# A two-layer decoder trunk: the router works on chunks of 128 neighbouring channels, its transposes stand between and behind the last output products, and its weights load from another queue

## What is computed

```
for l in range(DEPTH):                     # 2 layers
    h = rms_norm(x, norm_mix_g[l])
    x = x + token_mixers(h, ...)           # ends with merged @ w_out
    h = rms_norm(x, norm_ffn_g[l])
    glog = h @ rg_w + rg_b                 # 4 groups
    elog = h @ re_w + re_b                 # 32 experts, 8 in a group
    # best group, then the best two experts inside it; their weights from two softmaxes
    x = x + sum of w_e * (silu(h @ w_gate[e]) * (h @ w_up[e])) @ w_down[e] for the two experts
return rms_norm(x, norm_final_g)
```

## Time and profile before

| | us |
|---|---|
| median of 3 runs | 1450.69 (1449.82 to 1451.84) |
| the profiled execution, its own time | 1451.94 |
| its span, first to last instruction | 1450.2 |
| mixing half of layer 0, from the first `low` to the last add to x | 13.54 to 254.49 |
| router of layer 0, up to the gather of the first pair | 254.49 to 268.50 |
| experts of layer 0 | to about 720 |
| mixing half of layer 1, same marks | 729.76 to 970.99 |

### The profile page before, as it was taken

One profiled execution on the slowest core, in us unless ns is written; L12 is line 12 of the kernel. 1 busy time (PEld: TensorE's weight loads), 2 busy tenths in 40 slices (PEclk: granted clock), 3 DMA queues, 4 the chain that ended last, 5 costly groups with the idle time before them and its releaser, 6 DMA issues.

```text
span 1450.2 us, 17631 instructions
## 1 busy us (share of the span) xinstructions
PE 1391.4 (96%) x7295; PEld 837.9 (58%) x7295; DVE 559.5 (39%) x882; ACT 358.0 (25%) x532; POOL 6.3 (0%) x36
## 2 busy tenths in 40 slices
PE   6999999999999999999889999999999999999986
PEld 5899888644444444443378988885444444444432
DVE  6686645532222222221267757455222222222213
ACT  5554442311111111111155444431111111111101
POOL 0000000000000000000000000000000000000000
PEclk9999999999999999999989999999999999999998
DMA  7555757799999999999936457587999999999995
GB/s 273 191 193 177 256 204 279 285 422 421 421 421 422 420 421 422 420 421 421 404 133 218 157 192 269 195 335 286 421 421 421 421 421 421 421 421 420 421 421 212
DMA packets 101123, 490.18 MB, mean 338 GB/s; under 512 B 8716, under 2 KB 12084, under 8 KB 51892
## 3 DMA queue, kind: packets, MB, share of 16 engines
q1 hardware_dynamic: 99940, 488.72, 84.1%
q10 hardware_dynamic: 1104, 0.34, 0.1%
HBM read 487.98 MB, written 1.05 MB: 337 GB/s over the span
## 4 chain that ended last, share of the span: by engine, by line
PE 67%; SPq 18%; DVE 7%; DMA 4%; issue 2%; ACT 1%; DVEq 0%; ACTq 0%
PE psB L1619 20%; SPq L502 18%; PE psA L1367 13%; PE psB L1367 12%; PE psC L1630 10%; PE psA L1608 6%; DMA slot<-in_expert_w_down_dram 4%; DVE parts L926 2%; PE psA L1644 2%; PE psA L1645 1%; DVE score_work L1021 1%; DVE top L1020 1%; PE psD L1671 1%; ACT parts L731 1%; PE psC L1583 1%
## 5 line engine op out<-in xcount | busy, mean ns | idle before, releaser
L1619 PE MATMUL psB<-slot,uT 128*64 128x512 f32 x2048 | 460.0, 596 | 6.5 <-DMA slot<-in_expert_w_up_dram 6.5
L1619 PEld LDWEIGHTS psB<-slot,uT 128*64 128x64 f32 x2048 | 142.8, 137 | 275.1 <-issue 272.1
L1630 PE MATMUL psC<-slot,ybT_plain 128*64 128x512 f32 x1024 | 227.5, 596 | 3.9 <-ACT ybT_plain L839 2.7
L926 DVE TENSOR_TENSOR parts<-slot,parts 128x2048 fp32r<-128x2048 f32 (+1 forms) x80 | 177.4, 2249 | 70.2 <-ACT parts L731 69.9
L731 ACT ACTIVATE parts<-slot 128x2048 fp32r<-128x2048 f32 (+1 forms) x80 | 147.8, 1879 | 92.7 <-PE psA L1367 50.0
L1630 PEld LDWEIGHTS psC<-slot,ybT_plain 128*64 128x64 f32 x1024 | 71.1, 137 | 136.2 <-issue 129.3
L1242 DVE TENSOR_TENSOR x<-x,psA 128x1024 f32<-128x1024 f32 x62 | 75.7, 1221 | 190.2 <-PE psA L1645 190.2
L1367 PE MATMUL psB<-parts,hT_parts 128*128 128x512 f32 x448 | 138.9, 391 | 0.2
L1608 PEld LDWEIGHTS psA<-sel_mem,xn 128*128 128x128 f32 x1024 | 119.2, 192 | 27.0 <-issue 25.7
L1608 PE MATMUL psA<-sel_mem,xn 128*128 128x128 f32 x1024 | 127.4, 278 | 2.5 <-DVE sel_mem L1209 2.5
L1260 DVE TENSOR_TENSOR low_y_parts<-psC,low_y_parts 128x512 fp32r<-128x512 f32 x64 | 41.2, 686 | 223.7 <-ACT low_y_parts L842 223.7
(11 more groups left out here) (300 smaller groups left out, 1193.4 us busy)
## 6 DMA issues: line engine op xcount, KB each, us to landing
slot<-in_expert_w_gate_dram SPq DMA_DIRECT2D x128, 1024.0 KB, 23.1
slot<-in_expert_w_up_dram SPq DMA_DIRECT2D x128, 1024.0 KB, 22.4
slot<-in_expert_w_down_dram SPq DMA_DIRECT2D x128, 1024.0 KB, 24.3
slot<-in_w_in_dram SPq DMA_DIRECT2D x56, 1024.0 KB, 5.0
slot<-in_w_out_dram SPq DMA_DIRECT2D x8, 1024.0 KB, 4.9
slot<-in_w_proj_b_dram SPq DMA_DIRECT2D x4, 1024.0 KB, 5.0
slot<-in_w_proj_c_dram SPq DMA_DIRECT2D x4, 1024.0 KB, 5.0
slot<-in_w_proj_a_dram SPq DMA_DIRECT2D x4, 1024.0 KB, 4.9
```

The costliest lines, as they stand in the source:

```text
L926: v.tensor_tensor(low_part, mix_slot(i), high_part, ALU.subtract).then_inc(low_dve, 1)
L1619: ins = te.matmul(psB[j * BLK:(j + 1) * BLK, o, :], xT[:, 4 * half + c, j * BLK:(j + 1) * BLK], w[:, c, :], start=half == 0 and c == 0, st ...
L1630: ins = te.matmul(psC[j * BLK:(j + 1) * BLK, n, :], hidT[:, 2 * k + c, j * BLK:(j + 1) * BLK], w[:, c, n * 512:(n + 1) * 512], start=k == ...
```

## The change

It does four things.

1. **Chunks.** A chunk of the router is 128 neighbouring channels. The router's weights are loaded in that layout, `(c p) n` in place of `(p c) n`, which cuts each load into pieces of 4 or 32 numbers; before, a partition's piece was 8 times as long. The gain is multiplied into the router's weights `r_w` in `parameters()`, so that the copies out of PSUM are plain; for this the rows of `norm_ffn_g` come as a third small table.
2. **Loads.** `router_loads` is called by SP behind its sixth load of weights, and has seven DMAs; ACT issues none. The seven are waited for at the same place of `parameters()` as before.
3. **Sums.** x is added in four pieces, by half and token block, each as soon as its block of the output product is there.
4. **Transposes and products.** The 8 transposes of the first half of the channels stand between the token blocks of the last output product; 4 of t = 0 and 4 of t = 1 stand behind it, with the router's products in four groups among them. ACT makes four copies out of PSUM and DVE one. `spin` has 15 products in place of 14, and 4 more behind the ranking.

```diff
         for i in range(MIX_SLOTS):
             load_mix(i)
+            if l == 0 and i == RAWS - 1:
+                router_loads(sp)
...
-    def router_loads(act):
+    def router_loads(sp):
-            act.dma_start(g_ffn_all[:, :, :], norm_ffn_g.rearrange("l (p c) -> p l c", c=KC)).then_inc(router_landed, 16)
-            act.dma_start(rg_all..., router_group_w.rearrange("l (p c) n -> p l (c n)", c=KC)).then_inc(router_landed, 16)
-            act.dma_start(re_all..., router_expert_w.rearrange("l (p c) n -> p l (c n)", c=KC)).then_inc(router_landed, 16)
+            sp.dma_start(g_ffn_all[:, :, :], norm_ffn_g.rearrange("l (p c) -> p l c", c=KC)).then_inc(router_landed, 16)
+            for l in range(DEPTH):
+                sp.dma_start(rg_all[:, l], router_group_w.rearrange("l (c p) n -> l p c n", p=P)[l]).then_inc(router_landed, 16)
+                sp.dma_start(re_all[:, l], router_expert_w.rearrange("l (c p) n -> l p c n", p=P)[l]).then_inc(router_landed, 16)
...
 # DVE, parameters()
-        dve.wait_ge(router_landed, 16 * 5)
+        dve.wait_ge(router_landed, 16 * (3 + 2 * DEPTH))
-        v.tensor_copy(r_w[:, :, 0:NG], rg_all[:, bass.ds(l, 1), :, :].rearrange("p l c n -> p (l c) n"))
-        v.tensor_copy(r_w[:, :, NG:], re_all[:, bass.ds(l, 1), :, :].rearrange("p l c n -> p (l c) n"))
+        gain = cols[:, FFN_COLS + l * KC:FFN_COLS + (l + 1) * KC].unsqueeze(2)
+        v.tensor_tensor(r_w[:, :, 0:NG], rg_all[:, l], gain.to_broadcast([P, KC, NG]), ALU.mult)
+        v.tensor_tensor(r_w[:, :, NG:], re_all[:, l], gain.to_broadcast([P, KC, NE]), ALU.mult)
...
 # ACT, router_norm()
-        act.wait_ge(dve_out, (l + 1) * len(on_dve))
+        for t in range(NT):
+            act.wait_ge(routeT_ps, l * 5 + t + 1)
+            turned(psC[:, t, :], 0, 4, t)
+        act.wait_ge(x_mixed, l * 2 + 2)
         sc.activation(xn[:, 0:D], x[:, 0, :], ACT.Square, accum_out=ss[:, 0:1]).then_inc(ss_act, 1)
-        even_bank(psA, 0, hT, g_ffn)
+        turned(psD[:, 0, :], 4, 4, 0)
+        turned(psD[:, 1, :], 4, 2, 1)
         root_of(2)
-        even_bank(psB, 2, hT, g_ffn)
...
 # DVE, router_norm() and the adds
-        for b, ps in ((1, psA), (3, psB)):
-            v.tensor_tensor(hT[:, 2 * b:2 * b + 2, :], ps[:, 1, :]..., g_ffn[...]..., ALU.mult).then_inc(hT_dve, 1)
+        dve.wait_ge(routeT_ps, l * 5 + 5)
+        v.tensor_copy(hT[:, 6:8, P:S], psC[:, 0, 0:2 * P].rearrange("p (c s) -> p c s", c=2)).then_inc(routeT_dve, 1)
...
-            v.tensor_tensor(dst, dst, result(n)[:, :, :], ALU.add).then_inc(dve_out, 1)
+            dve.wait_ge(out_ps, l * 2 + half + 1)
+            v.tensor_tensor(dst[:, 0, :], dst[:, 0, :], (psA, psB)[n % 2][:, 0, :], ALU.add).then_inc(x_mixed, 1)
+            v.tensor_tensor(dst[:, 1, :], dst[:, 1, :], result(n)[:, 1, :], ALU.add).then_inc(dve_out, 1)
...
 # PE, inside the last output product, and behind it
+                if part == 1 and t == 0:
+                    ins.then_inc(out_ps, 1)
+                    if half == 1:
+                        pe.wait_ge(dve_out, ...)
+                        for u in range(NT):
+                            route_transposes(psC[:, u, :], range(4), u)
...
+        pe.wait_ge(x_mixed, l * 2 + 2)
+        route_transposes(psD[:, 0, :], range(4, 8), 0)
+        for t in range(NT):
+            pe.wait_ge(routeT_act, l * 4 + t + 1)
+            route(0, t)
+        pe.wait_ge(dve_out, (l + 1) * len(on_dve))
+        route_transposes(psD[:, 1, :], (4, 5), 1)
+        route_transposes(psC[:, 0, :], (6, 7), 1)
+        pe.wait_ge(routeT_act, l * 4 + 3)
+        route(1, 0).then_inc(route_ps, 1)
+        pe.wait_ge(routeT_act, l * 4 + 4)
+        pe.wait_ge(routeT_dve, l + 1)
+        route(1, 1).then_inc(route_ps, 1)
+        spin(15)
```

More of the change, by code:

```diff
@@ L275, in build_trunk @@
         thresholds = sb("thresholds", [P, S // BLK - 1])
-        rows = sb("rows", [DEPTH * (KC + CONV * 4), P])
-        cols = sb("cols", [P, DEPTH * (KC + CONV * 4)])
+        FFN_COLS = DEPTH * (KC + CONV * 4)
+        rows = sb("rows", [FFN_COLS + DEPTH * KC, P])
+        cols = sb("cols", [P, FFN_COLS + DEPTH * KC])
         g_mix = sb("g_mix", [P, KC])
@@ L383, in build_trunk @@
         vm_ps = sem("vm_ps")
+        out_ps = sem("out_ps")
+        routeT_ps = sem("routeT_ps")
         route_ps = sem("route_ps")
@@ L408, in build_trunk @@
         wsT_act = sem("wsT_act")
+        routeT_act = sem("routeT_act")
         route_exp = sem("route_exp")
@@ L440, in build_trunk @@
         merged_done = sem("merged_done")
+        x_mixed = sem("x_mixed")
+        routeT_dve = sem("routeT_dve")
         route_args = sem("route_args")
@@ L491, in sync_program @@
             sp.dma_start(rows[0:DEPTH * KC, :], norm_mix_g.rearrange("l (c p) -> (l c) p", p=P)).then_inc(rows_landed, 16)
-            sp.dma_start(rows[DEPTH * KC:, :], conv_w.rearrange("l k (c p) -> (l k c) p", p=P)).then_inc(rows_landed, 16)
+            sp.dma_start(rows[DEPTH * KC:FFN_COLS, :], conv_w.rearrange("l k (c p) -> (l k c) p", p=P)).then_inc(rows_landed, 16)
+            sp.dma_start(rows[FFN_COLS:, :], norm_ffn_g.rearrange("l (c p) -> (l c) p", p=P)).then_inc(rows_landed, 16)
             for l in range(DEPTH):
@@ L1382, in spin, with route_transposes, route, norm_transposes @@
                         te.matmul(psD[:, 1, 0:P], ones[:, :], before[:, :], start=True, stop=True)
-                def norm_transposes(which):
-                    if which == 0:
-                        pe.wait_ge(xn_act, l * 2 + 1)
-                        pe.wait_ge(xn_dve, l + 1)
-                    else:
-                        pe.wait_ge(dve_out, (l + 1) * len(on_dve))
+                def route_transposes(bank, cs, t):
+                    for k, c in enumerate(cs):
+                        ins = te.transpose(bank[:, k * P:(k + 1) * P], x[:, t, c * P:(c + 1) * P], ident[:, :])
+                    ins.then_inc(routeT_ps, 1)
+                def route(half, t):
+                    for c in range(4 * half, 4 * half + 4):
+                        ins = te.matmul(psB[:, t, 0:N_ROUTE], hT[:, c, t * P:(t + 1) * P], r_w[:, c, :],
+                                        start=c == 0, stop=c == KC - 1)
+                    return ins
+                def norm_transposes():
+                    pe.wait_ge(xn_act, l * 2 + 1)
+                    pe.wait_ge(xn_dve, l + 1)
                     for b in range(4):
@@ L1395, in norm_transposes @@
                             for t in range(NT):
-                                src = xn[:, t * D + m * P:t * D + (m + 1) * P] if which == 0 else x[:, t, m::KC]
+                                src = xn[:, t * D + m * P:t * D + (m + 1) * P]
                                 ins = te.transpose(ps[:, b % 2, c * S + t * P:c * S + t * P + P], src, ident[:, :])
@@ L1496, in spatial @@
                     ins.then_inc(vm_ps, 1)
-                norm_transposes(0)
+                norm_transposes()
                 group(G_QI)
@@ L1572, in tensor_program @@
                             ins.then_inc(mixed, 1)
-                norm_transposes(1)
-                for c in range(KC):
-                    if c % 4 == 0:
-                        pe.wait_ge(hT_act, l * 6 + 4 + c // 4 + 1)
-                    if c % 4 == 2:
-                        pe.wait_ge(hT_dve, l * 6 + 4 + c // 4 + 1)
-                    for t in range(NT):
-                        ins = te.matmul(psC[:, t, 0:N_ROUTE], hT[:, c, t * P:(t + 1) * P], r_w[:, c, :],
-                                        start=c == 0, stop=c == KC - 1)
-                ins.then_inc(route_ps, 1)
-                spin(14)
+                pe.wait_ge(x_mixed, l * 2 + 2)
+                route_transposes(psD[:, 0, :], range(4, 8), 0)
+                pe.wait_ge(layer_params, l + 1)
+                for t in range(NT):
[10 more added lines that the diff above has]
+                spin(15)
                 pe.wait_ge(members, l + 1)
@@ L1592, in tensor_program @@
                 ins.then_inc(rank_ps, 1)
+                spin(4)
                 def expert_arrived(i, p, tail):
```

36 lines of the change are left out of this document (15 added, 21 removed).

## The result

The changed kernel takes 1461.41 us (median of 4 executions, 1460.54 to 1462.24), the kernel before, run beside it, 1450.74 (4 executions, 1449.82 to 1451.84). The ratio is 1.0072, with a 95% interval of 1.0058 to 1.0087: slower by 10.7 us, where +14.1 was forecast. Its profiled execution took 1462.24, its span is 1460.5, which is 10.3 more than the span before.

A forecast was written before the change was run, and what follows sets the result against it. Mixing halves were taken as bound by PE and VectorE, the expert stage by its bytes behind a 9.90 us hole. Start +16.1 and routers -2.0 make +14.1 us, median 1464.8; range 1457.5 to 1475.5.

The forecast's parts named there:

- The mechanism: Program start: router loads queue behind six weight loads, VectorE waits ahead of low, PE follows 4.65 us behind, nothing catches up.
- the likeliest case: Whole kernel: start and router terms as summed, giving 1464.8 us; chance 0.45.
- the first rival: Program start: small packets take only what an engine needs, landing at 24.6, start +11.8, total 1460.5; chance 0.20.
- the clock rival: Gather and first products: the slow clock falls on them, 1.7 us more in each layer, total 1468.2; chance 0.13.
- The start: Program start: loads land at 28.9, so low starts at 29.6 in place of 13.54, +16.1 us.
- The router's packets therefore begin at about 22.0: SP's queue at the start: the router's packets begin once the weight bytes ahead are through, at about 22.0 us.
- 1.5 ns each: Router loads: time per packet, from 333 packets of 512 bytes queued behind a weight load; 6.9 us for 4608 packets.
- the lower bound: Router loads: least time per small packet, 0.55 ns over 16 engines, 2.6 us in all.
- 13 to 17 us from issue to landing: Sign in the changed trace: the router's loads in SP's queue take some 13 to 17 us from issue to landing.
- The router: Router stage: gains 1.0 us a layer, limited by ACT's chain, -2.0 for two layers; bounds -3.6 and 0.
- the 2.1 that was summed: Router on PE: the 16 passes of the first half's products take 2.1 us.
- the 0.24 us forecast: Last output product: inserted transposes make x complete at about 255.95 against 255.71, 0.24 us later.

The follow-up runs named there:

- e1: Changed kernel with VectorE's wait for the router loads, and the copies behind it, moved to just ahead of the adds to x; 1446.87 us, ratio 0.9971.
- e3: Kernel before with its five router loads, in the old large pieces, issued by SP behind the sixth weight load; 1461.62 us, ratio 1.0092.
- e5: e3 (old router and layout) with VectorE's wait for the router loads just ahead of the adds to x; 1446.55 us, ratio 0.9974.
- e4: e1 with ACT taking the exponentials between the two halves of xn, not behind both; 1444.75 us, ratio 0.9967.
- e7: e4 with 19 and 6 products without a use in the ranking, in place of 15 and 4; 1443.62 us, ratio 0.9956.
- e12: e5 with 24 products without a use ahead of layer 1's first transposes, the ranking's left at 14; 1447.6 us, ratio 0.9986.
- e2: Changed kernel with the seven router loads, in their new small pieces, issued by ACT at its start; 1459.5 us, ratio 1.0068.
- e8: e2 with VectorE's wait for the router loads put just ahead of the adds to x; 1452.09 us, ratio 1.0013.
- e11: e1 with 24 products without a use ahead of layer 1's first transposes, and 19 and 6 in the ranking; 1445.6 us, ratio 0.9964.
- e9: e7 with 24 products without a use ahead of layer 1's first transposes; 1444.57 us, ratio 0.9958.
- e10: e5 with 24 products without a use ahead of layer 1's first transposes, and 20 in the ranking in place of 14; 1450.73 us, ratio 0.9995.

## Why the prediction was right, and where its sizes were off

**The mechanism.** The wait ahead of `low`, the loads behind six weight loads in one queue, TensorE following 4.65 us behind `low`, and a mixing half that makes nothing up: all four are in the rows. e1 shows the cause by itself, since it moves nothing but the wait (with its copies). What came lies between the likeliest case (1464.8) and the first rival (cheap small packets, 1460.5), with one layer's share of the clock rival on top. That the total came within 3.4 us of the forecast is in part luck: the start was 2.75 us and the two routers 1.3 us better than summed, the experts 1.1, and a slow gather that was not in the sum took 1.6 back.

**The start, +16.1 forecast, +13.35 measured.** The landing was forecast for 28.9 and came at 26.1, and its working was off in three places, which partly cancel. First, "The router's packets therefore begin at about 22.0": they began at about 20. In the kernel before DMA all but stopped from 6.5 to 8 us (share 0.04 from 7.0 to 7.5); without ACT's small loads it doesn't (1.01 in the changed kernel, 1.00 in e3). The prediction named this effect and gave it half a microsecond at most. Second, "1.5 ns each" was the wrong row: in the bursts a packet took 0.72 and 0.76 ns, near the 0.55 of the lower bound, for which the first rival stood with its 0.20. Third, the sum has no term for SP's own issues. It took all seven loads for issued by the time the weights were through, but single issues took up to 4.09 us, the last ended at 23.38, and the second half of the packets came only then. (That they waited for SP is read from the pause; no run tests it alone. In e3 SP was through at 18.02, and the loads landed 2.85 us earlier.) So the 6.1 us from 20.0 to 26.1, for 4608 packets, are 3 us of packets, a pause of 1 us and 2.1 us to the end of the last loads; that this looks like 1.3 ns each is chance. The prediction's own sign for its mechanism, 13 to 17 us from issue to landing, failed by this too: it was 11.1 for the first load and 3.1 for the last. The VectorE part, 0.7 from landing to `low`, measured 0.79.

**The router, -1.0 a layer forecast, -1.42 and -1.87 measured.** The new limit was named rightly: ACT's chain of `xn`, table load and exponentials, and VectorE idles 1.01 us for it. The term that was off is when that chain starts. `xn` began 3.55 us behind the last add's end before (255.71 to 259.26) and begins 3.04 behind it now (269.48 to 272.52); the prediction left this distance about as it was. TensorE got from the first of 16 passes to the next transposes in 1.70 us (269.03 to 270.73), not the 2.1 that was summed, and it began 0.2 us ahead of VectorE's add (268.59 to 268.79), where the sum had both at 255.28. So VectorE's copy of 0.42 could start at 271.40, and the steps to rstd began at 271.74, 0.76 us behind the reciprocal in place of 1.27. The transposes cost more than the 0.24 us forecast: x was complete 0.42 later from `low` in layer 0, and 0.41 later in e1 than in e5, which both had layer 0's first group at the full clock. In layer 1 it was only 0.01 later, since the first group's slow stretch happened to be 0.39 shorter; without that the two layers gained the same, about 1.4.

**The slow clock on the gather**, a rival at 0.13, came true in one of two layers: 1.63 us, against the 1.7 forecast. e1 had it in layer 0 instead, e4 and e7 in neither. Nothing shows that the 8 transposes between the passes brought it: e3 and e12, which have none of them, show it too (their layer-1 gathers end 7.52 and 7.50 us behind `gsum`, against 5.90 before), and e2, e4, e8 and e11, which have them, show it in neither layer. What decides where the slow stretch falls stays open.

**Not forecast, and open:** -1.12 us in layer 0's experts. The kernels of this study, none of which touches that stage, lie between 455.8 and 457.45 us in it, the kernel before at the top. Nothing was tried on it.

## What to carry to other kernels

When a load moves back in a queue, look up where its wait stands: 10 to 13 us went into a wait some 240 us ahead of the first use of what it waited for, and moving the wait gave them all back. Small loads were cheap neither on a busy queue, whose bytes they stood behind, nor on a computing engine, which they held while it issued them; what was cheap is to need them late. When several steps feed one result, price the gain as far as the next of them: here ACT's exponentials took about a third of it (1.1 of 2.9 us in one layer, 0.75 of 2.6 in the other), and putting them between two copies that nobody awaited gave it back.

## What the runs showed of the hardware

- ACT was held for 2.39, 1.86 and 3.18 us by single issues of loads of 16, 128 and 4 KB while its queue held earlier small pieces (e2); SP's issues of the same loads took up to 4.09 us. The time of an issue did not follow the load's own size: the smallest load, a table of biases, was the longest on ACT.
- In the changed kernel small packets alone in SP's queue passed at 0.72 and 0.76 ns each over the 16 engines (2087 and 1969 in 1.5 us each).
- In e2, with both queues filled, 250 small packets and 249 large ones passed in the same microsecond, though the small ones' share was 14.8% and the large ones' 96.5%; from 4 to 5 us it was 1019 to 70.
- Which products met the 1.2 GHz clock changed from kernel to kernel with shifts of 1 or 2 us, at two places in each layer: the first group (7.2 us at the full clock, 8.5 to 9.5 with a slow stretch; slow in both layers of the kernel before and of the changed one, in neither of e5's), and the gather (1.63 us longer). The profiled execution of one kernel shows one such draw; a gain of 2 to 3 us in the stages was hidden by it in one pair (e1 and e5). 24 further products in the idle time ahead of layer 1's first group moved the slow stretch by a few products in e11 and e9, and in e10 and e12 the group was fast throughout, as it had been in e5 without them.
- At the program's start the granted clock doesn't tell this: it reads 1.00 from 18.2 to 21.0 us of the kernel before, while the first pair of products takes 0.88 us, as it does in layer 1 at a granted clock of 0.50 (734.4 to 737.0). The duration of a product of the same shape was the surer sign there.
